# Three engines' orders inside the expert tile: where the high halves, the low halves, the windows and the output rows stand

## The chip, the cores and the metric

The kernel runs on one core of a Trainium2 chip. The metric is the device time of one execution in microseconds (us). A core has a matrix engine (TensorE, PE in the profile; its weight loads are the row PEld), a vector engine (VectorE, DVE), a scalar engine (ScalarE, ACT), GpSimd (POOL) and SyncE (SP), which here issues the transfers. Each engine works through its own program in order and waits on semaphores for the others. Weights stream from HBM through 16 DMA engines into on-chip memory.

## The reference, cut to what matters

The reference is a transformer block with a mixture of experts, followed by two further layers. The part around the change is the mixture:

```python
for e in range(N_EXPERTS):                       # 32 experts
    a = jax.nn.silu(hf @ w_e_gate[e]) * (hf @ w_e_up[e])
    out = out + gates[:, e:e + 1] * (a @ w_e_down[e])
```

There are 256 tokens of width 1024, an expert has 512 hidden features, and each token has weight in two experts only. So 512 pairs of token and expert are to be computed, in float32.

## The kernel before, in words

The kernel sorts the 512 pairs by expert and visits the 32 experts as 32 *tiles*, the fullest first. Tile m has six weight *units* of 1024 KB: two halves of the gate weights, two of the up weights and two of the down weights. The first three tiles have two passes of 128 rows, tiles 3 to 6 one pass of 128 rows ("heavy"), and tiles 7 to 31 one pass of 64 rows ("light", `m >= HEAVY`).

A product in float32 is made of three (or, for a light gate or up product, two) products of rounded parts, so each unit goes through a chain:

- SP loads the unit into one of six buffers `raw`, once DVE is through with the unit six before (`load` waits on `lo_ready`).
- ACT copies `raw` to the high part `whi` (`hi`, line 1233), one of three buffers; it waits until PE has used the unit three before (`unit_used`).
- DVE subtracts to get the low part `wlo` (`lo`, line 1748).
- PE multiplies. `weights_in` waits for both parts.

The order on every engine is written out by hand. With u the number `p0 + 6 * m - 2`, PE's tile m is: gate unit u; the turning of tile m-1's hidden rows (`turn_hidden`, line 900); units u+1, u+2, u+3 (lines 863 and 864); then the down products of tile m-1 with units u+4 and u+5 (`down`, lines 932 to 934). `down` needs, beside its weights, `hid_l` of tile m-1.

The hidden rows of tile m-1 pass through four small steps after PE has turned them: `silu_turned` on ACT (line 1395), `hidden_turned` on DVE (line 1992), `hidden_high` on ACT (line 1412) and `hidden_low` on DVE (line 1999). Other small steps of ACT are `window`, which copies the rows of the next tile's tokens (line 1375, and 1983 on DVE), `y_there`, which takes the finished rows of tile m-2 out of the accumulators (line 1405; SP then stores them), and `gate_out` and `up_out` (lines 1385 and 1390), which take out the light products. ACT's and DVE's orders around `hi` and `lo` of the units u+2 to u+7 are `tile` in the two programs. From tile 9 on most tiles run in a hardware loop of two tiles a round; the names above keep their place in it.

Tile m's rows of PE and ACT in the trace begin with the first matmul of unit u. After the last tile ACT and DVE finish in a written-out tail, POOL gathers the stored rows, and the next layer starts.

Of the kernel before, what the change touches and what calls it, by code (L numbers as in the profile page):

```python
# [41 lines left out]
LOOP = 2  # L42
# [8 lines left out]
def passes(m):  # L51

    return (2 * m, 2 * m + 1) if m < TWICE else (m + TWICE,)
# [62 lines left out]
def build(nc, t, out):  # L116

    with ExitStack() as ctx:
# [248 lines left out]
        def usize(u):  # L367
            return units[u][1] * units[u][2] if units[u] else UNIT
# [854 lines left out]
        def _(act):  # L1223
            st = dict(hi=0, lin=0, step=0, split=0, want=0, norm=0, sums=0, top=moe)

            def hi(u, i=None, step=6):

                act.wait_ge(raw_landed[u % RAW],
                            (0 if i is None else i * (step // 6 * 16)) + 16 * (u // RAW + (u % RAW > 0)))
                if i is not None or u >= HL:  # L1230
                    act.wait_ge(unit_used, (0 if i is None else i * step) + (u - HL + 1))
                n = usize(u)
                nc.scalar.activation(whi[u % HL][:, 0:n], raw[u % RAW][:, 0:n], ACT.Copy).then_inc(hi_ready, 1)  # L1233
# [129 lines left out]
            def experts(p0):  # L1363
# [4 lines left out]
                def row_start(m, i=None):  # L1368
                    at = start_i[0:1, m:m + 1] if i is None else start_i[0:1, bass.ds(i * LOOP + m, 1)]
                    return act.value_load(at, min_val=0, max_val=PAIRS_OUT)  # L1370

                def window(s, m, row):

                    w = P if m < HEAVY else SLOTS
                    nc.scalar.activation(got_h[s % 2][:, :, 0:w], xc_h[:, :, bass.ds(row, w)],
                                         ACT.Copy).then_inc(win_h, 1)
# [10 lines left out]
                def up_out(u, s, i=None):  # L1387

                    act.wait_ge(unit_used, (0 if i is None else i * (6 * LOOP)) + u)
                    nc.scalar.activation(hid[s % 2], ps[:, 2 + s % 2, :], ACT.Copy).then_inc(pair_out, 1)  # L1390

                def silu_turned(s, i=None):

                    act.wait_ge(r_hid_mm, (0 if i is None else i * LOOP) + s + 1)
                    nc.scalar.activation(sil[s % 2][:, 0:256], ps[:, 6, 0:256], ACT.Silu).then_inc(r_silu, 1)

                def y_there(u, m, i=None):

                    act.wait_ge(unit_used, (0 if i is None else i * (6 * LOOP)) + u)
                    first, w = passes(m)[0], P if m < HEAVY else SLOTS  # L1400
                    for s in passes(m):
                        if s >= 2:
                            act.wait_ge(y_stored, (0 if i is None else i * (16 * LOOP)) + 16 * (s - 1))
                        at = 4 + 2 * (s - first)
                        nc.scalar.activation(y_out[s % 2][0:w, :], ps[0:w, at:at + 2, :].rearrange("p b n -> p (b n)"),
                                             ACT.Copy).then_inc(r_y, 1)

                def hidden_high(m, i=None):
                    add, first = 0 if i is None else i * LOOP, passes(m)[0]
                    if m >= HEAVY:  # L1410
                        act.wait_ge(r_hid, add + first + 1)
                        nc.scalar.activation(hid_h[first % 2][:, :, 0:SLOTS],
                                             hid[first % 2][:, 0:256].rearrange("p (k s) -> p k s", k=4),
                                             ACT.Copy).then_inc(r_hid_h, 1)
                        return
                    for s in passes(m):
                        act.wait_ge(r_hid_mm, add + s + 1)
                        nc.scalar.activation(hid_h[s % 2], ps[:, 6 + s - first, :].rearrange("p (k s) -> p k s", k=4),
                                             ACT.Copy).then_inc(r_hid_h, 1)
# [21 lines left out]
                def tile(m, i=None):  # L1441
                    if m < TWICE:
                        return tile_twice(m)
                    u, s, light = p0 + 6 * m - 2, passes(m)[0], m >= HEAVY
                    more = m < TILES - 1
                    if more:
                        row = row_start(s + 1, i)
                        window(s + 1, m + 1, row)
                    if not light:
                        y_there(u, m - 2)  # L1450
                    hi(u + 2, i, 6 * LOOP)
                    hi(u + 3, i, 6 * LOOP)
                    if m > HEAVY:
                        silu_turned(s - 1, i)
                    hi(u + 4, i, 6 * LOOP)
                    hidden_high(m - 1, i)
                    if light:
                        y_there(u, m - 2, i)
                    hi(u + 5, i, 6 * LOOP)
                    if light:  # L1460
                        gate_out(u + 3, s, i)
                    else:
                        silu(u + 3, s)
                    hi(u + 6, i, 6 * LOOP)
                    if light:
                        up_out(u + 4, s, i)
                    hi(u + 7, i, 6 * LOOP)

                for c in range(4):
# [23 lines left out]
                u = p0 + 6 * TILES  # L1493
# [141 lines left out]
            for half in range(2):  # L1635
                m = st["lin"] + half
# [47 lines left out]
            for a in range(4):  # L1684
                ahead(u_od[4 + a])
                m = st["lin"]
# [45 lines left out]
        def _(dve):  # L1732
# [9 lines left out]
            def lo(u, i=None, step=6):  # L1742

                dve.wait_ge(hi_ready, (0 if i is None else i * step) + (u + 1))
                if i is not None or u >= HL:
                    dve.wait_ge(unit_used, (0 if i is None else i * step) + (u - HL + 1))
                n = usize(u)
                v.tensor_tensor(wlo[u % HL][:, 0:n], raw[u % RAW][:, 0:n], whi[u % HL][:, 0:n].bitcast(F32),  # L1748
                                ALU.subtract).then_inc(lo_ready, 1)
# [219 lines left out]
            def experts(p0):  # L1969
# [8 lines left out]
                def window(s, m, row):  # L1978

                    if m < HEAVY:  # L1980
                        v.tensor_copy(got_l[s % 2], xc_l[:, :, bass.ds(row, P)]).then_inc(win_l, 1)
                    else:
                        v.tensor_copy(got_h[s % 2][:, :, SLOTS:], xc_l[:, :, bass.ds(row, SLOTS)]).then_inc(win_l, 1)
# [11 lines left out]
                def hidden_low(m, i=None):  # L1995
                    add, first = 0 if i is None else i * LOOP, passes(m)[0]
                    if m >= HEAVY:
                        dve.wait_ge(r_hid_h, add + first + 1)
                        v.tensor_tensor(hid_l[first % 2][:, :, 0:SLOTS],  # L1999
                                        hid[first % 2][:, 0:256].rearrange("p (k s) -> p k s", k=4),  # L2000
                                        hid_h[first % 2][:, :, 0:SLOTS].bitcast(F32), ALU.subtract).then_inc(r_hid_l, 1)
                        return
                    for s in passes(m):
                        dve.wait_ge(r_hid_h, add + s + 1)
                        v.tensor_tensor(hid_l[s % 2], ps[:, 6 + s - first, :].rearrange("p (k s) -> p k s", k=4),
                                        hid_h[s % 2].bitcast(F32), ALU.subtract).then_inc(r_hid_l, 1)
# [20 lines left out]
                def tile(m, i=None):  # L2027
                    if m < TWICE:
                        return tile_twice(m)
                    u, s = p0 + 6 * m - 2, passes(m)[0]  # L2030
                    more = m < TILES - 1
                    if more:
                        row = row_start(s + 1, i)
                    lo(u + 2, i, 6 * LOOP)
                    if m > HEAVY:
                        hidden_turned(s - 1, i)
                    lo(u + 3, i, 6 * LOOP)
                    lo(u + 4, i, 6 * LOOP)
                    hidden_low(m - 1, i)
                    lo(u + 5, i, 6 * LOOP)  # L2040
                    if more:
                        window(s + 1, m + 1, row)
                    if m < HEAVY:
                        dve.wait_ge(unit_used, u + 4)
                        hidden(s)
                    lo(u + 6, i, 6 * LOOP)
                    lo(u + 7, i, 6 * LOOP)
# [28 lines left out]
                u = p0 + 6 * TILES  # L2076
# [156 lines left out]
            for k, u in enumerate(u_br):  # L2233
# [5 lines left out]
                m = st["lin"]  # L2239
# [30 lines left out]
            m = st["lin"]  # L2270
# [55 lines left out]
            row = table_f[0:1, :]  # L2326
# [40 lines left out]
            for a, u in enumerate(u_ev):  # L2367
                ahead(u)
                m = st["lin"]
# [85 lines left out]
            for a in range(4):  # L2455
                u, m = u_od[a], st["lin"]
# [176 lines left out]
```

## Time and profile before

| what | us |
|---|---|
| median of 3 runs (1866.47 to 1870.46) | 1869.78 |
| the profiled execution's own time | 1866.47 |
| its span in the trace | 1864.1 |
| PE busy (matmul) / weight loads, whole span | 1698.9 / 1513.4 |
| DVE busy / ACT busy | 1296.8 / 1014.5 |
| transfers: mean rate over the span | 211 GB/s |

The span is what the rows add up to; the 2.4 us between it and the execution's own time lie around it. The page's forty slices of 46.6 us show that the expert stage differs from the rest: there the DMA row stands at 9 and the rate at 400 to 420 GB/s for ten slices, and ACT and DVE stand at 8 and 9 where they are at 3 to 6 elsewhere. Matmuls overlap, so a busy PE is not a PE at its peak. In a row of the timeline, the first number is the start and the second how long the instruction (or the run of like ones) took; in brackets stands how long its engine had been idle and who ended that. The time from one start to the next on an engine is often 0.1 us shorter than the duration, since instructions overlap slightly.

### The profile page before, as it was taken

To read this page: it belongs to the slowest core of one execution; us is meant where nothing else is said; L and a number is where in the kernel's file an instruction comes from. 1 tells how busy PE (TensorE), PEld (TensorE's weight loads), DVE (VectorE), ACT (ScalarE), POOL (GpSimd) and SP (SyncE) were. 2 spreads that over 40 slices of the span, in tenths; PEclk is the share of its full clock that TensorE was granted. 3 is DMA by queue.
4 is the path that set the end of the run, shared out by engine and by line. 5 is a ranking of instruction groups with operands and counts; after the bars stand their busy time and mean duration, and the time that the engine had idled before them with its cause. 6 is when DMAs were issued, how large, how long until landed. Compare 5 with 4: busy or idle time off the path is not lost. (4 is left out here: it accounts for less than half of the span.)

```text
span 1864.1 us, 29897 instructions
## 1 busy us (share of the span) xinstructions
PE 1698.9 (91%) x11504; PEld 1513.4 (81%) x11504; DVE 1296.8 (70%) x1448; ACT 1014.5 (54%) x1106; POOL 55.6 (3%) x56
## 2 busy tenths in 40 slices
PE   8999988899999999999957698899999889899998
PEld 7998868778876666666636598799999889799997
DVE  6455687665788999999947856576556867676554
ACT  4333566355688888888842444354334474353333
POOL 0000000000000000000031300000000010000000
PEclk9998999899999999999978799999999989999999
DMA  9651114176799999999972334246554535336540
GB/s 326 186 182 57 37 67 140 51 275 219 265 400 419 419 420 420 419 407 415 406 277 62 96 114 159 91 154 203 184 181 146 165 124 176 113 114 204 180 158 23
DMA packets 195504, 393.96 MB, mean 211 GB/s; under 512 B 6961, under 2 KB 152113, under 8 KB 179025
## 3 DMA queue, kind: packets, MB, share of 16 engines
q1 hardware_dynamic: 193744, 386.11, 57.1%
q0 software_dynamic: 1664, 6.52, 1.0%
q8 instruction: 66, 1.08, 0.2%
q14 instruction: 30, 0.24, 0.0%
HBM read 379.77 MB, written 12.85 MB: 211 GB/s over the span
## 5 line engine op out<-in xcount | busy, mean ns | idle before, releaser
L1748 DVE TENSOR_TENSOR wlo<-raw,whi 128x2048 fp32r<-128x2048 f32 (+2 forms) x358 | 811.0, 2273 | 276.4 <-ACT whi L1233 271.4
L1233 ACT ACTIVATE whi<-raw 128x2048 fp32r<-128x2048 f32 (+2 forms) x358 | 673.3, 1889 | 365.0 <-PE ps L628 256.8
L626 PE MATMUL ps<-xh,whi 128*128 128x256 f32 x1080 | 317.6, 294 | 35.6 <-DVE xl L1761 33.0
L627 PE MATMUL ps<-xl,whi 128*128 128x256 f32 x1080 | 311.3, 288 | 0.0
L628 PE MATMUL ps<-xh,wlo 128*128 128x256 f32 x1080 | 311.1, 288 | 0.0
L626 PEld LDWEIGHTS ps<-xh,whi 128*128 128x128 f32 x1080 | 212.4, 197 | 42.3 <-issue 37.9
L626 PE MATMUL ps<-xb_h,whi 128*128 128x256 f32 x768 | 218.6, 285 | 5.3 <-DVE arena L1830 5.3
L628 PE MATMUL ps<-xb_h,wlo 128*128 128x256 f32 x768 | 218.0, 284 | 0.0
L627 PE MATMUL ps<-xb_l,whi 128*128 128x256 f32 x768 | 218.0, 284 | 0.0
L627 PEld LDWEIGHTS ps<-xl,whi 128*128 128x128 f32 x1080 | 212.9, 197 | 0.4
L628 PEld LDWEIGHTS ps<-xh,wlo 128*128 128x128 f32 x1080 | 212.4, 197 | 0.1
L863 PE MATMUL ps<-whi,xh 128*128 128x512 f32 x400 | 159.3, 398 | 1.4 <-DVE wlo L1748 1.2
L864 PE MATMUL ps<-wlo,xh 128*128 128x512 f32 x400 | 156.4, 391 | 0.0
L626 PEld LDWEIGHTS ps<-xb_h,whi 128*128 128x128 f32 x768 | 148.2, 193 | 5.8 <-DVE arena L1830 5.7
L627 PEld LDWEIGHTS ps<-xb_l,whi 128*128 128x128 f32 x768 | 148.2, 193 | 0.1
L628 PEld LDWEIGHTS ps<-xb_h,wlo 128*128 128x128 f32 x768 | 148.1, 193 | 0.0
L932 PE MATMUL ps<-whi,ah 128*64 128x512 f32 (+1 forms) x280 | 111.4, 398 | 29.1 <-DVE al L1999 27.8
L626 PE MATMUL ps<-ah,whi 128*128 128x256 f32 (+2 forms) x428 | 122.2, 285 | 2.5 <-DVE al L1761 2.5
L627 PE MATMUL ps<-al,whi 128*128 128x256 f32 (+2 forms) x428 | 121.6, 284 | 0.0
L628 PE MATMUL ps<-ah,wlo 128*128 128x256 f32 (+2 forms) x428 | 121.5, 284 | 0.0
L934 PE MATMUL ps<-whi,al 128*64 128x512 f32 (+1 forms) x280 | 110.4, 394 | 0.0
L933 PE MATMUL ps<-wlo,ah 128*64 128x512 f32 (+1 forms) x280 | 110.2, 393 | 0.0
(348 smaller groups left out, 2736.6 us busy)
## 6 DMA issues: line engine op xcount, KB each, us to landing
raw<-w_e_gate_dram SPq DMA_DIRECT2D x64, 1024.0 KB, 8.2
raw<-w_e_up_dram SPq DMA_DIRECT2D x64, 1024.0 KB, 8.5
raw<-w_e_down_dram SPq DMA_DIRECT2D x64, 1024.0 KB, 8.1
raw<-ffn_w_gate_up_dram SPq DMA_DIRECT2D x44, 1024.0 KB, 5.1
raw<-w_in_dram SPq DMA_DIRECT2D x30, 1024.0 KB, 5.5
raw<-ffn_w_down_dram SPq DMA_DIRECT2D x22, 1024.0 KB, 5.0
raw<-xa_w_kv_dram SPq DMA_DIRECT2D x16, 1024.0 KB, 5.3
raw<-xa_w_q_dram SPq DMA_DIRECT2D x8, 1024.0 KB, 5.0
```

What stands on the lines that cost most here:

```text
L626: mm = nc.tensor.matmul(o, wh, h, start=first and a == 0, stop=False, skip_group_check=not group)
L627: nc.tensor.matmul(o, wh, l, start=False, stop=False, skip_group_check=not group)
L628: mm = nc.tensor.matmul(o, wl, h, start=False, stop=last and a == len(parts) - 1, skip_group_check=not group)
L863: nc.tensor.matmul(o, hl[:, k, :], wh[:, k, :], start=first and k == 0, stop=False)
L864: mm = nc.tensor.matmul(o, hl[:, k, :], wl[:, k, :], start=False, stop=last and k == 3)
L932: nc.tensor.matmul(o, h, wh[:, k, cols], start=half == 0 and k == 0, stop=False)
L933: nc.tensor.matmul(o, h, wl[:, k, cols], start=False, stop=False)
L934: mm = nc.tensor.matmul(o, l, wh[:, k, cols], start=False, stop=half == 1 and k == 1)
L1233: nc.scalar.activation(whi[u % HL][:, 0:n], raw[u % RAW][:, 0:n], ACT.Copy).then_inc(hi_ready, 1)
L1748: v.tensor_tensor(wlo[u % HL][:, 0:n], raw[u % RAW][:, 0:n], whi[u % HL][:, 0:n].bitcast(F32), ALU.subtract).then_inc(lo_ready, 1)
```

## The change

In ACT's `tile`, `y_there` now comes first for every tile (before, light tiles did it behind `hidden_high`), `silu_turned` moves from behind `hi(u + 3)` to before it, `hidden_high` from behind `hi(u + 4)` to before it, the gate's step (`gate_out` or `silu`) from behind `hi(u + 5)` to before it, the up step from behind `hi(u + 6)` to before it, and `window` from the very start to between `hi(u + 6)` and `hi(u + 7)`. In DVE's `tile`, `hidden_low` moves from behind `lo(u + 4)` to before it, and `window` from behind `lo(u + 5)` to before it. PE's, SP's and POOL's programs are the same. No work is added or removed.

```diff
--- before.py
+++ after.py
@@ -1445,25 +1445,23 @@
                     more = m < TILES - 1
                     if more:
                         row = row_start(s + 1, i)
-                        window(s + 1, m + 1, row)
-                    if not light:
-                        y_there(u, m - 2)
+                    y_there(u, m - 2, i)
                     hi(u + 2, i, 6 * LOOP)
-                    hi(u + 3, i, 6 * LOOP)
                     if m > HEAVY:
                         silu_turned(s - 1, i)
+                    hi(u + 3, i, 6 * LOOP)
+                    hidden_high(m - 1, i)
                     hi(u + 4, i, 6 * LOOP)
-                    hidden_high(m - 1, i)
-                    if light:
-                        y_there(u, m - 2, i)
-                    hi(u + 5, i, 6 * LOOP)
                     if light:
                         gate_out(u + 3, s, i)
                     else:
                         silu(u + 3, s)
-                    hi(u + 6, i, 6 * LOOP)
+                    hi(u + 5, i, 6 * LOOP)
                     if light:
                         up_out(u + 4, s, i)
+                    hi(u + 6, i, 6 * LOOP)
+                    if more:
+                        window(s + 1, m + 1, row)
                     hi(u + 7, i, 6 * LOOP)
 
                 for c in range(4):
@@ -2035,11 +2033,11 @@
                     if m > HEAVY:
                         hidden_turned(s - 1, i)
                     lo(u + 3, i, 6 * LOOP)
+                    hidden_low(m - 1, i)
                     lo(u + 4, i, 6 * LOOP)
-                    hidden_low(m - 1, i)
-                    lo(u + 5, i, 6 * LOOP)
                     if more:
                         window(s + 1, m + 1, row)
+                    lo(u + 5, i, 6 * LOOP)
                     if m < HEAVY:
                         dve.wait_ge(unit_used, u + 4)
                         hidden(s)
```

One light tile on ACT, from its start. `whi<-raw` is `hi` (units u+2 to u+7 in turn), `scr<-ps 128x256` is `silu_turned`, `ah<-scr` is `hidden_high`, `arena<-ps` is `y_there`, the two `scr<-ps 128x512` are `gate_out` and `up_out`, and `xh<-xc_h` is `window`. Before:

```order
L1375 ACTIVATE xh<-xc_h_49 128x8x64
L1233 ACTIVATE whi2<-raw2 128x2048
L1233 ACTIVATE whi0<-raw3 128x2048
L1395 ACTIVATE scr<-ps 128x256
L1233 ACTIVATE whi1<-raw4 128x2048
L1412 ACTIVATE ah<-scr 128x4x64
L1405 ACTIVATE arena<-ps 128x1024
L1233 ACTIVATE whi2<-raw5 128x2048
L1385 ACTIVATE scr<-ps 128x512
L1233 ACTIVATE whi0<-raw0 128x2048
L1390 ACTIVATE scr<-ps 128x512
L1233 ACTIVATE whi1<-raw1 128x2048
```

And of the changed kernel, the same tile:

```order
L1405 ACTIVATE arena<-ps 128x1024
L1233 ACTIVATE whi2<-raw2 128x2048
L1395 ACTIVATE scr<-ps 128x256
L1233 ACTIVATE whi0<-raw3 128x2048
L1412 ACTIVATE ah<-scr 128x4x64
L1233 ACTIVATE whi1<-raw4 128x2048
L1385 ACTIVATE scr<-ps 128x512
L1233 ACTIVATE whi2<-raw5 128x2048
L1390 ACTIVATE scr<-ps 128x512
L1233 ACTIVATE whi0<-raw0 128x2048
L1375 ISA
L1375 ACTIVATE xh<-xc_h_49 128x8x64
```

The output rows went to the head and the window to the end (one `hi` follows it), and each of the small steps between went ahead of one `hi`.

The same light tile on DVE, where `wlo<-raw,whi` is `lo`, `scr<-ps,scr` is `hidden_turned`, `al<-scr,ah` is `hidden_low` and `xh<-xc_l` is the window. Before:

```order
L1748 TENSOR_TENSOR wlo2<-raw2,whi2 128x2048
L1992 TENSOR_TENSOR scr<-ps,scr 128x256
L1748 TENSOR_TENSOR wlo0<-raw3,whi0 128x2048
L1748 TENSOR_TENSOR wlo1<-raw4,whi1 128x2048
L1999 TENSOR_TENSOR al<-scr,ah 128x4x64
L1748 TENSOR_TENSOR wlo2<-raw5,whi2 128x2048
```

And of the changed kernel (its lines are two lower):

```order
L1746 TENSOR_TENSOR wlo2<-raw2,whi2 128x2048
L1990 TENSOR_TENSOR scr<-ps,scr 128x256
L1746 TENSOR_TENSOR wlo0<-raw3,whi0 128x2048
L1997 TENSOR_TENSOR al<-scr,ah 128x4x64
L1746 TENSOR_TENSOR wlo1<-raw4,whi1 128x2048
L1981 ISA
```

The hidden rows' low part now stands ahead of the low half of unit u+4, and the window ahead of that of unit u+5.

## Rows read from the trace of the kernel before

**Rows 1.** Windows: us, busy time (and count) by engine, granted clock, DMA share, GB/s.

```profile
600.00:900.00 300.00, 280.52 (x1359) 204.57 (x1359) 273.52 (x171) 267.53 (x228) 0.00 (x0) 1.00 1.02 417
949.00:953.00 4.00, 3.88 (x11) 2.12 (x11) 2.29 (x1) 1.21 (x1) 0.00 (x0) 0.58 0.98 325
```

**Rows 2.** Waits from 600 to 900: us in total, times, longest.

```profile
PEld ps L932 <- DVE al L1999: 27.2, 19, 1.5
...
ACT whi L1233 <- PE ps L864: 26.3, 19, 1.5
...
ACT whi L1233 <- DMA raw<-w_e_up_dram: 0.4, 1, 0.4
```

**Rows 3.** DMA issues from 600 to 900: count, size of each, median us to landing.

```profile
raw<-w_e_gate_dram SPq DMA_DIRECT2D x37, 1024.0 KB, 8.1
compact_y<-arena SPq DMA_DIRECT2D x19, 256.0 KB, 7.0
```

**Rows 4.** Timeline of ACT in one light tile (start, duration, instruction, idle before).

```profile
704.71 3.75 ACT L1233 ACTIVATE whi<-raw 128x2048 fp32r<-128x2048 f32 x2 [0.31 <-PE ps L934]
708.36 0.37 ACT L1395 ACTIVATE scr<-ps 128x256 f32<-128x256 f32 x1
710.17 1.93 ACT L1233 ACTIVATE whi<-raw 128x2048 fp32r<-128x2048 f32 x1 [1.45 <-PE ps L864]
712.00 0.40 ACT L1412 ACTIVATE ah<-scr 128x256 fp32r<-128x256 f32 x1
712.30 1.01 ACT L1405 ACTIVATE arena<-ps 64x1024 f32<-64x1024 f32 x1
713.21 1.90 ACT L1233 ACTIVATE whi<-raw 128x2048 fp32r<-128x2048 f32 x1
```

**Rows 5.** Timeline of DVE in the same tile.

```profile
706.75 2.29 DVE L1748 TENSOR_TENSOR wlo<-raw,whi 128x2048 fp32r<-128x2048 f32 x1 [0.45 <-ACT whi L1233]
708.96 0.42 DVE L1992 TENSOR_TENSOR scr<-ps,scr 128x256 f32<-128x256 f32 x1
709.29 2.28 DVE L1748 TENSOR_TENSOR wlo<-raw,whi 128x2048 fp32r<-128x2048 f32 x1
712.22 2.29 DVE L1748 TENSOR_TENSOR wlo<-raw,whi 128x2048 fp32r<-128x2048 f32 x1 [0.65 <-ACT whi L1233]
714.43 0.42 DVE L1999 TENSOR_TENSOR al<-scr,ah 128x256 fp32r<-128x256 f32 x1
```

**Rows 6.** Timeline of PE: that tile's first matmul, first down matmul, next tile's first.

```profile
704.51 0.40 PE L863 MATMUL ps<-whi,xh 128*128 128x512 f32 x1
...
714.90 0.45 PE L932 MATMUL ps<-whi,ah 128*64 128x512 f32 x1 [1.12 <-DVE al L1999]
...
720.47 0.39 PE L863 MATMUL ps<-whi,xh 128*128 128x512 f32 x1
```

**Rows 7.** Timeline of PE: starts of the turning, in tiles 8, 9, 10 and 31.

```profile
562.65 1.11 PE L900 MATMUL ps<-arena,scr 128*128 128x64 f32 x9
...
578.55 0.89 PE L900 MATMUL ps<-arena,scr 128*128 128x64 f32 x7
...
595.03 1.00 PE L900 MATMUL ps<-arena,scr 128*128 128x64 f32 x8
...
929.41 0.78 PE L900 MATMUL ps<-arena,scr 128*128 128x64 f32 x6
```

**Rows 8.** Timeline of ACT at the end of the expert stage.

```profile
940.60 1.92 ACT L1233 ACTIVATE whi<-raw 128x2048 fp32r<-128x2048 f32 x1 [1.89 <-DMA raw<-w_e_down_dram]
...
945.61 0.38 ACT L1395 ACTIVATE scr<-ps 128x256 f32<-128x256 f32 x1 [0.31 <-PE ps L900]
945.89 1.00 ACT L1405 ACTIVATE arena<-ps 64x1024 f32<-64x1024 f32 x1
947.99 0.42 ACT L1412 ACTIVATE ah<-scr 128x256 fp32r<-128x256 f32 x1 [1.09 <-DVE scr L1992]
```

**Rows 9.** Timeline of PE: the first matmul of the last down product.

```profile
949.12 0.41 PE L932 MATMUL ps<-whi,ah 128*64 128x512 f32 x1 [3.55 <-DVE al L1999]
```

## The prediction

> **What bounds the kernel now.** The change touches only the tiles of the expert stage from the fourth on, and its steady part is the light tiles, so I read one long window there first. Over 600 to 900 us all four resources look full at once [rows 1]: PE 280.5 of 300 us, DVE 273.5, ACT 267.5, and the 16 DMA engines at a share of 1.02 while they move 417 GB/s. A share cannot say which of them sets the pace; the waits can [rows 2]. In these 19 tiles PE waited 27.2 us for `hidden_low` (weight loads of the down product, 1.4 us a tile), ACT waited 26.3 us for PE at one place (the same 19 times), and ACT waited for a weight transfer once, for 0.4 us. So the transfers are full but just in time, and the pace is set by a loop through three engines. One tile shows it. Count from T, the tile's first matmul at 704.51 [rows 6]:
>
> - PE does unit u, the turning and unit u+1; that frees the buffer that `hi(u+4)` waits for, at T+5.66, where ACT had stood for 1.45 us [rows 4].
> - `lo(u+4)` starts 2.05 us later, at T+7.71, `hidden_low` 2.21 us after that, at T+9.92 [rows 5].
> - PE's down product starts when `hidden_low` is done, at T+10.39, and its two units take 5.57 us to the next tile's first matmul, at T+15.96 [rows 6].
>
> DVE does `hidden_low` last, directly behind `lo(u+4)`, and both are needed by the same down product. That order can't be improved by swapping the two unless the chain in front of them gets earlier.
>
> **The change in a light tile.** I lay the new order out with the distances between starts in the same rows.
>
> - `y_there` goes first. It starts where `hi(u+2)` did, at T+0.20 (both wait for the last down product), and takes 0.91 us to the next start (712.30 to 713.21). `hi(u+2)` is at T+1.11, `lo(u+2)` 2.04 us later (704.71 to 706.75), at T+3.15, and DVE is free of it at T+5.36.
> - `silu_turned` waits for PE's turning. It ran at 708.36, T+3.85, directly behind two `hi`; in the new order ACT is free at T+1.11+1.83 = T+2.94 (half of 3.75 less the overlap) and stands until the turning is done. Its start cannot move up by more than a tenth or two: the turning is 16 matmuls behind unit u. I take T+3.85. So 0.9 us of ACT's time, which held `hi(u+3)` before, is now idle.
> - `hi(u+3)` comes behind it. `silu_turned` costs 0.28 us to the next start (945.61 to 945.89) [rows 8]: T+4.13, where it had been at about T+2.03. `lo(u+3)` follows 2.05 us later, T+6.18; it was at T+4.78. `hidden_turned` (T+5.36 to T+5.69) fits in front. This is the step that costs: 1.40 us on DVE's chain.
> - `hidden_high` at T+4.13+1.83 = T+5.96, 0.30 us, then `hi(u+4)` at T+6.26 instead of T+5.66. PE frees its buffer at T+5.66, so 0.6 us later than it could.
> - DVE: `lo(u+3)` to T+8.39, `hidden_low` 0.33 us, `lo(u+4)` at T+8.72 (its high part is there at T+8.31), done 2.29 us later at T+11.01. PE's down product starts at T+11.06 with 0.05 us as before. Before it was T+10.39: **+0.67 us a tile**. It will wait for the low part of the weights, no longer for `hidden_low`, which is there since T+8.81.
> - Behind that nothing gives time back. The down products still take 5.57 us, and the next tile starts at T+16.63. PE also waits in front of unit u+3, which needs `lo(u+3)` (ready T+8.47, while PE is free near T+7.2), but is through with it at about T+10.4, before T+11.06. `lo(u+5)`, behind the window, starts at T+11.27 and is done at T+13.56; the second down unit starts at T+13.7, so it is covered by 0.15 us only. If this cover fails, a tile costs a few tenths more. The window on ACT stands between `hi(u+6)` and `hi(u+7)`, near T+13.0, and is needed at T+16.6. The moved `gate_out` and `up_out` wait for units u+2 and u+3 of this tile; they still leave `hi(u+6)` at T+11.2 with `lo(u+6)` at T+13.5 and needed at T+16.6. These edits I cost at nothing; the 5.57 us of down products hide them.
>
> No stall in a store: `y_there` of tile m needs the store two before, issued more than a tile earlier, and stores land in 7.0 us [rows 3].
>
> **The heavy tiles (3 to 6).** There `y_there` was already first, and a tile has a fuller PE. `hidden_low` before `lo(u+4)` delays the latter by at most one small operation. I take 0 and keep -1 to +1 us for all of them. Tile 7 has no `silu_turned`; 0 too.
>
> **The sum.** The turning starts at 562.65 in tile 8 and at 929.41 in tile 31 [rows 7], 24 starts in all, so 23 periods in 366.76 us, 15.95 each. One of these (578.55 to 595.03) took 16.48 us, 0.5 more than the rest; the transfers held it up, and with a loop of 16.6 us they would not. With tile 31 itself there are 24 tiles at +0.67 us, 16.1 us, less that 0.5, is 15.6 us.
>
> At the end something comes back. There `hi` of the last down units waited 1.89 us for its transfer, and after the last `silu_turned` (945.61) ACT waited 1.09 us for `hidden_turned`, which stood behind the late `lo` [rows 8]; PE started at 949.12, 3.51 us after 945.61 [rows 9]. In the longer loop the transfers are early, and the path is `silu_turned` 0.28, `y_there` 0.91, and `hidden_high` to PE 1.13 (947.99 to 949.12): 2.32 us. That returns 1.2 us. Everything behind (store, gather, next layer) follows from there unchanged. The net is 15.6 - 1.2 = **14.4 us**. Against the profiled execution's own 1866.47 us this is 1880.9; that execution was the fastest of the three, and from the median of 1869.78 it is 1884.2. I forecast **1884 us**.
>
> Bounds: the 0.67 us consists of starts that agree within 0.1 us over the tiles. If `silu_turned` could start 0.2 us earlier it is 0.47 (24 tiles: 11.3 us, less 1.7: about 10); if the cover of `lo(u+5)` fails by 0.2 us it is 0.87 (about 19). With the heavy tiles' 1 us, and up to 1.6 us if the slow matmuls after 949 (below) went away, 7 to 20 us: 1877 to 1890. From the 3.3 us between the profiled run and the median comes more, and I give 1876 to 1892.
>
> **The rivals.**
>
> *The transfers set the pace anyway, so nothing changes.* A light tile moves six units of 1024 KB and a store of 256 KB [rows 3], 6.55 MB, which at 417 GB/s takes 15.7 us, a quarter of a microsecond less than the tile takes now. If DMA were the bound, both orders would hide behind it, and the time would be 1870. For it speaks the share of 1.02, and that the landing takes 8.1 us; against it that ACT waited once in 19 tiles, and that my new loop is 0.9 us longer than these 15.7. It decides if the order's cost is under 0.1 us. Chance 0.07.
> The Trainium skill ("DMA: Bandwidth & Descriptors", section "Where 436 GB/s comes from") says that loads from HBM are bound at about 358 GB/s by the HBM side, 435 being the ceiling of the fabric. By 358 a tile could not be shorter than 18.3 us and this rival would be certain; the trace has 417 GB/s over 300 us [rows 1], so here the measurement decides against the 358.
>
> *Faster: `hidden_low` was the last thing that PE waited for and is moved ahead.* It will be there at about T+8.8, and if `lo(u+4)` were early as well, down could start when PE is through with unit u+3, 1.1 us earlier. The transfers allow only 15.7 of it: 23 periods by 0.25 us is 5.8 us, and the end of the stage already waits for its transfer, so 1 to 6 us, 1867. It decides if `lo(u+4)` ends before T+10.3, for which `lo(u+3)` would have to start by T+5.5; that is before its high part exists, since `hi(u+3)` now stands behind the turning. Chance 0.03.
>
> *Slower by far: the clock of PE falls.* PE now waits in two places of a tile, 1.3 and 0.7 us. After 3.55 us of waiting [rows 9] the granted clock was 0.58 over 949 to 953, partly at the lower of the two levels (1.2 GHz), while with 1.5 us a tile it stayed at 1.00 for 300 us [rows 1]. In that stretch 11 matmuls started in 4 us, against 17 to 18 at 0.23 us each, so about 1.6 us are lost an event; in 24 tiles 38 us on top, 1922. It decides if the two waits together are enough. Chance 0.04.
> The Trainium skill ("TensorE: Matmul & The Clock Gate", section "What's actually happening") has the chip set the clock by how busy PE has been of late; the 0.58 after the long wait agrees, and what waits of a light tile's length do, beyond the 1.5 us that left it at 1.00, no row here shows.
>
> *Another loop*: a cover that I cost at nothing fails in every tile (`lo(u+5)`, or `hi(u+7)` behind the window), +0.5 us a tile, 12 us on top, 1896. Chance 0.06.
>
> **How the numbers follow.** The forecast's own case has 0.80. What a measurement of this kernel can tell from no change is about 0.2%, 3.7 us. Slower: 0.80 + 0.04 + 0.06 = 0.90; the same 0.07; faster 0.03. The range 1876 to 1892 is the likeliest case's own and leaves out about 0.17.
>
> **What would show it.** Right: the turning comes every 16.6 us; the wait of PE at line 932 is put down to DVE `wlo`, not `al`; a second wait of about a microsecond stands before a unit at line 863, for `wlo`; ACT's idle time at `hi(u+4)` is gone and about 0.9 us of idle stands before `silu_turned`, released by PE at line 900; the DMA share in the light tiles falls to about 0.98 and 400 GB/s, and ACT waits for no weights at the end. Wrong: a period of 15.9 us or less, a `lo(u+3)` that starts within 5 us of the tile's first matmul, or a granted clock under 1.00 in 600 to 900.

## The result, and the profile after

The changed kernel takes 1887.75 us (median; 1887.12 to 1890.71) against 1870.46 us before (1866.47 to 1872.59): a ratio of 1.0091, with a 95% interval of 1.0073 to 1.0108. It is slower by 17.3 us. The prediction had 1884 us, in 1876 to 1892, from a step of 14.4 us.

The profiled execution has a span of 1882.7 us, 18.6 more than before. First the same window of the light tiles as in [rows 1]:

```profile
600.00:900.00 300.00, 273.92 (x1290) 192.95 (x1289) 259.41 (x163) 255.93 (x215) 0.00 (x0) 1.00 1.00 393
```

In 300 us PE starts 1290 matmuls instead of 1359, ACT and DVE each stand some 12 to 14 us longer, and the transfers bring 393 GB/s instead of 417. The granted clock is 1.00 as before. Nothing is busier than it was; everything waits more. The waits of the same window, against [rows 2]:

```profile
DVE wlo L1746 <- ACT whi L1233: 42.0, 55, 1.5
...
PE ps L863 <- DVE wlo L1746: 13.9, 18, 0.8
...
PE ps L932 <- DVE wlo L1746: 11.9, 18, 0.7
ACT scr L1395 <- PE ps L900: 11.2, 17, 0.7
ACT arena L1405 <- PE ps L934: 9.2, 10, 0.9
ACT arena L1405 <- DMA compact_y<-arena: 7.4, 8, 0.9
```

The wait of PE for `hidden_low` (`al`) is gone. In its place stand two, in each of 18 tiles: at line 863, 0.8 us, and at line 932, 0.7 us, both for a low half of weights (`wlo`). ACT waits 0.7 us in front of `silu_turned` (line 1395) for the turning. The last two lines are one wait: in all 18 tiles `y_there` starts 0.12 us behind the end of the last down matmul, and the store that the second of them names had landed some 15 us before. One light tile shows the chain; first ACT, whose rows of before are [rows 4]:

```profile
712.72 1.02 ACT L1405 ACTIVATE arena<-ps 64x1024 f32<-64x1024 f32 x1 [0.92 <-PE ps L934]
713.64 1.90 ACT L1233 ACTIVATE whi<-raw 128x2048 fp32r<-128x2048 f32 x1
716.20 0.38 ACT L1395 ACTIVATE scr<-ps 128x256 f32<-128x256 f32 x1 [0.67 <-PE ps L900]
716.48 1.91 ACT L1233 ACTIVATE whi<-raw 128x2048 fp32r<-128x2048 f32 x1
718.32 0.42 ACT L1412 ACTIVATE ah<-scr 128x256 fp32r<-128x256 f32 x1
718.64 1.90 ACT L1233 ACTIVATE whi<-raw 128x2048 fp32r<-128x2048 f32 x1
```

DVE in the same tile, against [rows 5]:

```profile
715.65 2.29 DVE L1746 TENSOR_TENSOR wlo<-raw,whi 128x2048 fp32r<-128x2048 f32 x1 [1.54 <-ACT whi L1233]
717.86 0.42 DVE L1990 TENSOR_TENSOR scr<-ps,scr 128x256 f32<-128x256 f32 x1
718.51 2.29 DVE L1746 TENSOR_TENSOR wlo<-raw,whi 128x2048 fp32r<-128x2048 f32 x1 [0.23 <-ACT whi L1233]
720.72 0.42 DVE L1997 TENSOR_TENSOR al<-scr,ah 128x256 fp32r<-128x256 f32 x1
721.05 2.29 DVE L1746 TENSOR_TENSOR wlo<-raw,whi 128x2048 fp32r<-128x2048 f32 x1
```

And PE, against [rows 6]: the tile's first matmul, its turning, unit u+3, the first down matmul, and the next tile's first.

```profile
712.43 0.40 PE L863 MATMUL ps<-whi,xh 128*128 128x512 f32 x1
...
714.27 1.89 PE L900 MATMUL ps<-arena,scr 128*128 128x64 f32 x16
...
720.95 0.47 PE L863 MATMUL ps<-whi,xh 128*128 128x512 f32 x1 [0.80 <-DVE wlo L1746]
...
723.69 0.42 PE L932 MATMUL ps<-whi,ah 128*64 128x512 f32 x1 [0.66 <-DVE wlo L1746]
...
729.23 0.40 PE L863 MATMUL ps<-whi,xh 128*128 128x512 f32 x1
```

Read along: ACT stands until the turning is through (716.20), then `silu_turned`, and only then `hi` of unit u+3 (716.48). DVE's `lo` of it starts at 718.51, `hidden_low` at 720.72, `lo` of unit u+4 at 721.05, done at 723.34, and PE starts down at 723.69. The hidden rows, which PE waited for before, were there at 721.14.

In what follows times in a tile are counted from the start of the turning (line 900), because it is easy to find in every trace. A round of the loop is two tiles, so most distances alternate between two values up to 0.1 us apart (the first down matmul of the changed kernel between 9.32 and 9.42). In the light tiles the period, taken over 18 tiles, went from 15.91 to 16.74 us, and the first down matmul (median) from 8.52 to 9.37 us behind the turning. The turning of tile 8 starts at 563.61 and that of tile 31 at 948.36, against [rows 7]:

```profile
563.61 1.56 PE L900 MATMUL ps<-arena,scr 128*128 128x64 f32 x13
...
948.36 0.89 PE L900 MATMUL ps<-arena,scr 128*128 128x64 f32 x7
```

The end of the expert stage on ACT, against [rows 8]:

```profile
959.27 1.92 ACT L1233 ACTIVATE whi<-raw 128x2048 fp32r<-128x2048 f32 x1 [1.62 <-DMA raw<-w_e_down_dram]
961.91 1.92 ACT L1233 ACTIVATE whi<-raw 128x2048 fp32r<-128x2048 f32 x1 [0.72 <-DMA raw<-w_e_down_dram]
964.92 0.38 ACT L1395 ACTIVATE scr<-ps 128x256 f32<-128x256 f32 x1 [1.09 <-PE ps L900]
```

and on PE, against [rows 9]:

```profile
967.65 0.42 PE L932 MATMUL ps<-whi,ah 128*64 128x512 f32 x1 [2.77 <-DVE al L1997]
```

The last units' transfers were late here too, and from the last `silu_turned` to PE it took 2.73 us, against 3.51 before.

### The profile page after: what moved, and what is told of

Read it like the earlier page. It is cut to its first block and busy times, and to the rows that moved or that the text cites. A ratio compares the mean times of both kernels' runs of the same rounds, so it can differ in the third digit from the quotient of the medians.

```text
span 1882.7 us, 29957 instructions
## 1 busy us (share of the span) xinstructions
PE 1708.2 (91%) x11504; PEld 1512.0 (80%) x11504; DVE 1296.3 (69%) x1448; ACT 1016.9 (54%) x1106; POOL 55.6 (3%) x56
## 5 line engine op out<-in xcount | busy, mean ns | idle before, releaser
L863 PEld LDWEIGHTS ps<-whi,xh 128*128 128x128 f32 x400 | 75.1, 188 | 54.4 <-ACT whi L1233 30.6
```

Source lines behind the costliest of these rows:

```text
L863: nc.tensor.matmul(o, hl[:, k, :], wh[:, k, :], start=first and k == 0, stop=False)
```

## The experiments

Each ran beside the kernel before on the same chip. `hi`, `lo` and the units have the names of the code above. The differences in microseconds given below are between medians.

**e1: ACT's new order, DVE's old.** The edit, from the changed kernel, in DVE's `tile`:

```diff
                     lo(u + 3, i, 6 * LOOP)
-                    hidden_low(m - 1, i)
                     lo(u + 4, i, 6 * LOOP)
+                    hidden_low(m - 1, i)
+                    lo(u + 5, i, 6 * LOOP)
                     if more:
                         window(s + 1, m + 1, row)
-                    lo(u + 5, i, 6 * LOOP)
```

> ACT's new order with DVE's old one. Chain theory: hi(u+3) still stands behind the turning, so lo(u+3) starts 4.19 us after the turning's start as in the changed kernel. lo(u+4) follows at 6.40 and hidden_low at 8.61, done at 9.03. PE now waits for hidden_low and starts its down product about 0.05 us behind it, as in the kernel before, at 9.1, against 9.42 in the changed kernel and 8.56 before. The period is then about 16.4 us (changed 16.73, before 15.95), 24 x 0.46 = 11 us less 1 at the end: 10 us slower than before. Rival (DVE's order is what costs, since the hidden rows' low part pushes the weights' low part back): this kernel is as fast as before, period 15.9.

Measured: 1879.43 against 1868.92 us, ratio 1.006 (1.004 to 1.008), 10.5 us slower than before. Period 16.49 us, PE's down product 9.08 us behind the turning (9.1 expected). DVE and PE in one tile whose turning starts at 714.83:

```profile
719.07 4.49 DVE L1746 TENSOR_TENSOR wlo<-raw,whi 128x2048 fp32r<-128x2048 f32 x2 [0.23 <-ACT whi L1233]
723.48 0.42 DVE L1997 TENSOR_TENSOR al<-scr,ah 128x256 fp32r<-128x256 f32 x1
```

```profile
723.96 0.45 PE L932 MATMUL ps<-whi,ah 128*64 128x512 f32 x1 [0.35 <-DVE al L1997]
```

ACT's order by itself costs 10.5 of the 17 us. `lo(u+3)` starts as late as in the changed kernel (4.20 us behind the turning, by the median), and here PE starts 0.06 us behind `hidden_low` (723.90). The rival falls: with DVE's old order the loss is still there.

**e2: DVE's new order, ACT's old.** The edit, from the kernel before:

```diff
                     lo(u + 3, i, 6 * LOOP)
+                    hidden_low(m - 1, i)
                     lo(u + 4, i, 6 * LOOP)
-                    hidden_low(m - 1, i)
-                    lo(u + 5, i, 6 * LOOP)
                     if more:
                         window(s + 1, m + 1, row)
+                    lo(u + 5, i, 6 * LOOP)
```

> ACT's old order with DVE's new one. Chain theory: hidden_high still follows hi(u+4) and is done 6.1 us after the turning's start, so hidden_low starts at 6.1, lo(u+4) at 6.45 (5.9 before), done at 8.74, and PE starts down at about 9.05, with the 0.3 us that it took behind a wlo in the changed kernel. That is 0.49 us a tile more than before, period 16.4, and about 11 us slower than before. Rival (ACT's order alone costs): as before, 15.95.

Measured: 1880.3 against 1868.92 us, ratio 1.007 (1.0051 to 1.009), 11.4 us slower. Period 16.44, down 9.06 us behind the turning (9.05 expected). DVE:

```profile
716.97 0.42 DVE L1999 TENSOR_TENSOR al<-scr,ah 128x256 fp32r<-128x256 f32 x1 [0.83 <-ACT ah L1412]
717.32 2.29 DVE L1748 TENSOR_TENSOR wlo<-raw,whi 128x2048 fp32r<-128x2048 f32 x1
```

`hidden_low` now stands in front of `lo(u+4)` and waits 0.83 us for `hidden_high`, which ACT does behind `hi(u+4)`. The weights' low half waits behind both. So either half of the change costs some 10 to 11 us alone, and both together 17: they put two delays on one chain, and overlap in part.

**e3: the changed kernel with `silu_turned` put back.**

```diff
-                    if m > HEAVY:
-                        silu_turned(s - 1, i)
                     hi(u + 3, i, 6 * LOOP)
+                    if m > HEAVY:
+                        silu_turned(s - 1, i)
```

> The changed kernel, with silu_turned put back behind hi(u+3); all else as changed. Chain theory: hi(u+3) starts 1.2 us after the turning's start instead of 2.21, silu_turned at 3.03 instead of 1.93; hidden_turned is done at 3.98, lo(u+3) starts at 3.90 instead of 4.19, hidden_low at 6.11, lo(u+4) at 6.44, done at 8.73, PE's down product at 9.05 instead of 9.42. Period 16.35 us, 0.38 less than changed: 9 us faster than the changed kernel, 8 to 9 slower than before. Rival (the moved y_there and window cost the time, silu_turned is free since ACT stood anyway): no change from the changed kernel, period 16.7.

Measured: 1879.19 against 1868.92 us, ratio 1.006 (1.0038 to 1.0082), 10.3 us slower than before, so some 7 us of the 17 are gone. Period 16.43 (16.35 expected), down at 9.05, as expected. By the medians of 18 tiles `hi(u+3)` starts 1.17 us behind the turning's start instead of 2.21, and `lo(u+3)` at 3.88 instead of 4.19. The step of the prediction is shown: the small operation stood waiting, and what stood behind it paid.

The 10.3 us that are left have a place in the trace too. `lo(u+3)` starts at 3.88 and not at 2.92 as in the kernel before, and `lo(u+2)` at 1.34 and not at 0.38: the 0.9 us of `y_there` at the head, which the wait for the turning covers in the changed kernel, now push the chain. e7 below bears this out: it differs from e3 only in the places of `y_there`, the windows and the light products' steps, and its period is 0.59 us shorter. No run here takes these apart.

**e4: the changed kernel with PE's waits in another order.**

```diff
-                    weights_in(u, i, 6 * LOOP)
                     if half == 0:
                         pe.wait_ge(r_hid_l, add + last + 1)
                         if first >= 1:
                             pe.wait_ge(r_y, add + first)
+                    weights_in(u, i, 6 * LOOP)
```

> The changed kernel; in PE's down product the waits stand in another order: first for the hidden rows' low part and for the output rows, then for the weights. Nothing else differs. In the changed kernel PE started 0.31 to 0.35 us behind the end of lo(u+4), against 0.05 us behind hidden_low before and 0.15 behind lo(u+3) where the weights are waited for last. If the hand-off is long because two more waits are passed after the one that ends last, PE starts at 9.15 after the turning instead of 9.42, the period is 16.5 (0.25 less) and the time 6 us less than the changed kernel's. Rival (a hand-off from DVE's long subtraction simply takes longer than one from a short one): period 16.73, no change.

Measured: 1881.28 against 1868.92 us, ratio 1.0075 (1.0049 to 1.0101), 12.4 us slower than before, some 5 less than the changed kernel. Period 16.54, 0.20 less. DVE's and PE's rows for the down product of one tile:

```profile
717.40 2.28 DVE L1746 TENSOR_TENSOR wlo<-raw,whi 128x2048 fp32r<-128x2048 f32 x1
```

```profile
719.83 0.42 PE L932 MATMUL ps<-whi,ah 128*64 128x512 f32 x1 [0.45 <-DVE wlo L1746]
```

PE starts 0.15 us behind the end of `lo(u+4)` at 719.68, where the changed kernel took 0.35 (723.34 to 723.69). All rows of ACT and DVE up to there are where they were (`lo(u+4)` at 6.74 behind the turning in both). So the order in which PE asks its semaphores is worth 0.2 us a tile here, and the rival (a long subtraction hands over more slowly) falls, since the producer is the same. The trace's records of PE's wait steps show why. In the changed kernel the low half is the first of four steps, which start at 723.38, 723.49, 723.58 and, with the weight load, 723.66. In e4 only the weight load is left behind it (719.72, then 719.80). In the kernel before, the wait for `hidden_low` was the last of the four and stood on the weight load itself (714.90), which is why that hand-off was 0.05 us.

**e5 and e6: the two edits that were costed at nothing.** e5 takes `y_there` from the head of a light tile and puts it behind `hi(u+4)`:

```diff
-                    y_there(u, m - 2, i)
+                    if not light:
+                        y_there(u, m - 2)
                     hi(u + 2, i, 6 * LOOP)
...
                     hi(u + 4, i, 6 * LOOP)
                     if light:
+                        y_there(u, m - 2, i)
                         gate_out(u + 3, s, i)
```

> The changed kernel with y_there of the light tiles taken from the head of the tile and put behind hi(u+4). If the prediction is right that the 0.9 us of y_there at the head are covered by the wait for the turning, silu_turned still starts 1.93 us after the turning's start, lo(u+3) at 4.19, PE's down product at 9.3 to 9.4, and the period stays at 16.73 us (within 0.1). Rival (y_there at the head delays the chain through hi(u+2) and lo(u+2)): the period falls by up to 0.9 us, to 15.9.

e6 puts ACT's window back at the head:

```diff
                         row = row_start(s + 1, i)
+                        window(s + 1, m + 1, row)
                     y_there(u, m - 2, i)
...
                     hi(u + 6, i, 6 * LOOP)
-                    if more:
-                        window(s + 1, m + 1, row)
                     hi(u + 7, i, 6 * LOOP)
```

> The changed kernel with ACT's window back at the start of the tile, its first instruction. Prediction: it costs nothing in either place, since ACT waits for PE's last down product at the head and for hi(u+7)'s buffer at the end: period 16.73 us (within 0.1). Rival (the window at the end delays hi(u+7), and so lo(u+7) and the next tile): a period that is 0.2 to 0.5 us shorter.

One execution each, 1888.82 and 1881.49 us, which says little; the periods say it: 16.75 and 16.74 us against 16.74. In e5 `lo(u+2)` starts a microsecond earlier (0.37 us behind the turning's start, not 1.35), but `silu_turned` at 1.93, `lo(u+3)` at 4.19 and `lo(u+4)` at 6.74 are unmoved. Both edits are free in the changed kernel's order, as said. The tiles ahead of the light ones differ from run to run by more than the edits could do (the turning of tile 8 starts at 564.76 in e5 and 561.31 in e6), so single times are no measure here.

**e7: the kernel before, with the hidden rows' halves ahead of `hi(u+4)` and `lo(u+4)`.**

```diff
                     if m > HEAVY:
                         silu_turned(s - 1, i)
-                    hi(u + 4, i, 6 * LOOP)
                     hidden_high(m - 1, i)
+                    hi(u + 4, i, 6 * LOOP)
...
                     lo(u + 3, i, 6 * LOOP)
-                    lo(u + 4, i, 6 * LOOP)
                     hidden_low(m - 1, i)
+                    lo(u + 4, i, 6 * LOOP)
```

> The kernel before with two edits alone: hidden_high ahead of hi(u+4) on ACT and hidden_low ahead of lo(u+4) on DVE. silu_turned stays behind hi(u+3). Chain theory: hi(u+4) stays at 3.83 us after the turning's start, since PE frees its buffer only then, and hidden_high (from 3.05 on) fits in front of it; hidden_low starts at 5.1 and lo(u+4) at 5.83 as before, done at 8.12; PE's down product at 8.41 with 0.29 us of hand-off, against 8.52 before. Period 15.8, so 0 to 3 us faster than before, no more than the transfers allow (6.55 MB a tile at 417 GB/s are 15.7 us, and the end of the stage waits for its last transfer): the same within 0.2 per cent. Rival (hidden_low ahead of lo(u+4) costs 0.34 us of DVE in any order of ACT, as in e2): period 16.3 to 16.4, 8 to 11 us slower than before.

Measured: 1866.92 against 1867.98 us, ratio 0.9985 (0.9973 to 0.9998). Period 15.84, down at 8.47 (8.41 expected). The same edit on DVE that cost 11 us in e2 costs nothing here. It was never the place of `hidden_low` alone, but that it waited there for ACT.

**e8: e7 with PE's waits in the order of e4.**

> e7 with PE's waits in the down product in the order of e4 (weights last). Chain theory: PE's down product at 8.22 us after the turning's start, 0.3 less than before, and engines alone would give a period of 15.6. If the transfers bound the stage from there, as they did in the earliest light tiles, the period is 15.7, ACT waits for transfers in many tiles (hi behind a raw buffer), and the time is 0 to 4 us less than before: the last units land no earlier. Rival (the transfers have slack, and the rate of 417 GB/s is only what the engines asked for): 24 x 0.3 = 7 us faster than before.

Measured: 1865.06 against 1867.98 us, ratio 0.9979 (0.9963 to 0.9995). Down at 8.28, period 15.65. Window and one wait of 600 to 900:

```profile
600.00:900.00 300.00, 285.12 (x1378) 208.06 (x1376) 278.76 (x174) 274.76 (x231) 0.00 (x0) 1.00 1.02 420
```

```profile
ACT whi L1233 <- DMA raw<-w_e_up_dram: 1.5, 5, 0.4
```

ACT at the end of the stage:

```profile
934.28 1.91 ACT L1233 ACTIVATE whi<-raw 128x2048 fp32r<-128x2048 f32 x1 [3.54 <-DMA raw<-w_e_down_dram]
```

Of the 7 us that the loop could give (24 x 0.3), some 3 arrived in the time. The tiles do come faster, but ACT waits for transfers five times instead of once, and for 3.54 us at the end: the turning of tile 31 is at 923.42, 6 us earlier than before, and the last one at 943.03, only 0.65 us earlier than the 943.68 before. The landings show the bound. In e8 one unit of every tile is copied 0.10 us behind its landing until 798 us; in the kernel before that ends at 627 us, and from there the smallest distance of a tile grows to over 3 us. So in the light tiles the transfers had a quarter of a microsecond a tile of slack, which e8 uses up, and at the end they cost what the tiles had gained. The 7 us of the rival did not come; e9 asks whether the end took them.

**e9: e8 with POOL's three loads for the next stage later.** e10 is the same edit on the kernel before. (Both wait for the last expert unit's landing in POOL's program.)

```diff
             pool.wait_ge(win_l, PASSES - 2)
+            u = moe + 6 * TILES - 1
+            pool.wait_ge(raw_landed[u % RAW], 16 * (u // RAW + (u % RAW > 0)))
             pool.dma_start(mem, kview(t["memT"])).then_inc(second_landed, 16)
```

> e8, and POOL issues its three transfers for the next stage (1.85 MB) only when the last expert unit has landed, and not after the last window. In the kernel before they share the DMA engines with the last down units, and ACT waited 1.89 us for one of these. If the end of the expert stage is bound by transfers, the last unit lands up to 1.85 MB / 417 GB/s = 4.4 us earlier, and this kernel is 3 to 6 us faster than e8. Rival (the end is bound by the engines' chain): no change from e8.

> The kernel before with the POOL edit of e9 alone. ACT no longer waits for the last down unit. The path from the last silu_turned to PE's last down product shortens from 3.51 to about 2.3 us, and the slow matmuls behind it (granted clock 0.58 in 949 to 953) may go: 1 to 3 us faster than before. Rival (the late transfer is covered by the chain anyway): no change in the 3.51 us.

e9: 1860.17 against 1867.72 us, ratio 0.996 (0.9946 to 0.9974), 7.6 us faster than before and by that 4.6 us faster than e8 (3 to 6 expected). The last turning starts at 938.30 instead of 943.03 in e8. It is the fastest version here.

e10: 1866.32 against 1867.72 us, ratio 1.0 (0.9989 to 1.0011): no difference, where 1 to 3 us were expected. The wait that the edit aims at is gone, though. ACT's and PE's rows at the end, and a window behind:

```profile
946.16 0.38 ACT L1395 ACTIVATE scr<-ps 128x256 f32<-128x256 f32 x1 [2.51 <-PE ps L900]
```

```profile
948.46 0.66 PE L932 MATMUL ps<-whi,ah 128*64 128x512 f32 x1 [2.34 <-DVE al L1999]
```

```profile
950.00:954.00 4.00, 4.00 (x10) 2.01 (x9) 1.87 (x1) 0.09 (x1) 0.00 (x0) 0.50 1.06 366
```

The path took 2.30 us instead of 3.51, just as worked out, but then the clock was granted at 0.50, its lower level, for the whole of 950 to 954, where [rows 1] have 0.58 for 949 to 953 before. From the last turning to the start of the last `y_there` it took 12.73 us (12.77 before). What the shorter wait gave the slower matmuls took back. In e9, with 2.14 us of waiting in front of the same down product, the granted clock was 1.00 over 942 to 950, and that stretch is 9.82 us (938.30 to 948.12). So nearly 3 of e9's 7.6 us lie there: 1.41 us in the path from `silu_turned` to PE (2.10 against 3.51 before) and 1.54 us behind it (5.79 against 7.33), where the clock did not fall. In e8 the wait was the same 2.14 us and the clock 0.51 over 946 to 950; there PE had stood 3.41 us in front of a down unit just before, and the clock had already been 0.65 over 938 to 942. What made e9 differ from e10, which had no such wait, is open.

## Why the prediction was right

The mechanism held step by step, and the sign, the place and the size followed. In the changed kernel's trace, counted from the tile's first matmul at 712.43: `silu_turned` at +3.77 (predicted 3.85), `hi(u+3)` at +4.05 (4.13), `lo(u+3)` at +6.08 (6.18), `hidden_low` at +8.29 (8.39), `lo(u+4)` at +8.62 (8.72), and done at +10.91 (11.01). Each is a tenth earlier than predicted: `silu_turned`, which had stood behind two `hi`, now started as soon as the turning was through, and the prediction had allowed it a tenth or two.

Then one term was too small. PE started down at +11.26, not +11.06. I took 0.05 us for the hand-off, from the kernel before, where PE waited for `hidden_low`; behind the weights' low half it is 0.35 us in this tile and 0.34 to 0.38 us in every one of the 18. e4 shows where it comes from. So a tile costs 0.83 us more (15.91 to 16.74), not 0.67. The sum by its terms, with the starts of the turning in tiles 8 and 31, the last turning (943.68 and 962.99) and the last `y_there` (956.45 and 974.96):

| term | predicted | measured |
|---|---|---|
| up to tile 8 | 0 | +0.96 |
| 23 periods | +14.9 | +17.99 |
| tile 31 | +0.67 | +0.36 |
| behind the last turning | -1.2 | -0.80 |
| sum | 14.4 | 18.5 |

The first is within what tile 8's start differs between runs (561.3 to 566.5 in these traces), so whether the heavy tiles gain or lose stays open.

That the time fell inside the range is in part luck. The range's upper side was reasoned from the cover of `lo(u+5)` failing by 0.2 us, which would have made a tile 0.87 us longer. The cover held, and the hand-off brought 0.83 us instead. The range's share is also a little off: the four rivals have 0.20 together, and the prediction says that about 0.17 lie outside.

At the end the prediction was wrong in a step, though not by much. It said that in the longer loop the transfers would be early. They were not: ACT waited 1.62 and 0.72 us for the last two down units, while 1.89 and 0.38 before. POOL's three loads start with the last window (at 943.82, and 925.37 before), a tile before the end, whatever the pace of the tiles, and share the DMA engines with just these units. In the kernel before, e10 removes that and the wait with it. Of the 1.2 us that the prediction gave back here, 0.8 came.

The costless edits were costless (e5, e6), though only under the wait for the turning, as e3 against e7 shows, and the cover of `lo(u+5)`, which I gave only 0.15 us, held: from the down product's start to the next tile it took 5.54 us (723.69 to 729.23), as long as before.

On the rivals. *Transfers set the pace*: no for this change, since the loop of 16.7 us is longer than the transfers' 15.7, but e8 reaches that bound: a period of 15.65 us, 420 GB/s, a unit in most tiles that is used as it lands, and gains that are lost at the end. The Trainium skill's 358 GB/s ("DMA: Bandwidth & Descriptors", section "Where 436 GB/s comes from"), which it works out as a stack's rate shared by two cores, is passed in every window of the light tiles read here (393 to 420 GB/s, with one core at work), the 435 in none. *Faster*: `hidden_low` was early, as that rival has it, but `lo(u+4)` was not, and the point from which it decides (`lo(u+3)` by T+5.5) was missed by 0.6 us; in e7, where it starts 2.9 us behind the turning, the swap does no harm, and what it gains is 1 us. *The clock*: 1.00 over 600 to 900 with waits of 0.8 and 0.7 us in every tile, so no. *A cover fails*: no.

## What to carry to other kernels

A small operation that waits for another engine did better here behind the long independent work than in front of it: on an engine that works in order, whatever stands behind the wait pays for it, and here it was the head of the next chain. An edit that such a wait covers is free only as long as the wait is there (`y_there` at the head). Before a producer is moved ahead of its neighbour, look whether its own inputs are there by then; the same swap on DVE cost 11 us with ACT's old order and nothing with the other. And when a wait changes over from one semaphore to another, take the hand-off from a row that waits for the same one, or count how many waits stand behind it.

## What the runs showed of the hardware

- PE's start behind a release depends on where the releasing wait stands among its waits. With three steps behind it (the last is the weight load) it took 0.34 to 0.38 us in the 18 light tiles of the changed kernel, with one 0.15 in those of e4, with the same producer; on the weight load itself 0.05 (the kernel before, another producer). The last two tiles are written out, not looped, and ask in another order: there it took 0.10 us behind the low half (changed kernel, one step behind it) and 0.25 behind `hidden_low` (before, two steps).
- The granted clock undid a gain: e10 shortened PE's wait to 2.34 us, but 10 matmuls started in the 4 us from 950 at a clock of 0.50; in the kernel before it was 13 in 950 to 954 at 0.62. Behind a wait of 2.14 us it was 1.00 in e9 and 0.51 in e8. The length of the last wait alone does not tell the clock behind it.
- A share of 1.02 of the DMA engines was no bound by itself (before, ACT waited for weights 0.4 us in 19 tiles, and units lay ready up to 3 us before they were used), but it had only a quarter of a microsecond a tile left, which e8 used up.
